# One Trainium2 core, a four-branch mixer and a two-layer block: sums, splits, bias tables and banks moved, and the gated recurrence written in another order

## The chip, the cores and the metric

The kernel runs on one core of one Trainium2 chip. The metric is the device time of one execution in microseconds (us). Within a core five engines run their own instruction queues side by side: PE (matrix multiply), DVE (vector), ACT (scalar, activations), POOL (GpSimd) and SP (here used for weight loads). They meet at semaphores. ACT, POOL and SP can also issue DMA transfers; in the profile such issues stand on ACTq, POOLq and SPq.

## The reference

The input is 256 tokens by 1024 channels, all in float32. Two blocks follow each other.

```python
# first block
h = rmsnorm(x)
z, xbc, dt, b_qkv, c_qkv, c_f, d_q, d_kv, gates = split(h @ w_in)
y_a = mamba2(z, silu(conv4(xbc)), dt)        # decays: exp(cumsum_t - cumsum_s), s <= t
y_b = moba(b_qkv, rel_bias)                  # softmax(q k / 8 + bias[t - s]) v, causal
y_c = forgetting(c_qkv, c_f)                 # softmax(q k / 8 + cum_t - cum_s) v, causal
y_d = sliding_window(d_q, d_kv, sinks, rel_bias)   # window 128, own bias
x = x + (sum_i sigmoid(gates_i) * (y_i @ w_branch_i)) @ w_out
x = x + (silu(h @ w_gate) * (h @ w_up)) @ w_down   # h = rmsnorm(x), width 2816
# second block
x = x + hgrn2(rmsnorm(x));  x = x + swiglu(rmsnorm(x))
y, u = split(rmsnorm(x) @ lru_w_in)          # 1024 and 1024 columns
uc = conv4(u)                                # causal, 4 taps
r, i = sigmoid(uc @ wa + ba), sigmoid(uc @ wx + bx)     # 4 diagonal blocks of 256
a = exp(-8 r softplus(-lam));  b = sqrt(1 - a*a) * (i * uc)
hs = scan(a, b)                              # hs[t] = a[t] hs[t-1] + b[t]
x = x + (hs * gelu(y)) @ lru_w_out
x = x + swiglu(rmsnorm(x));  out = rmsnorm(x)
```

## The kernel before

**Weights and their splitting.** Each float32 product is made of three products in the fast format fp32r: high part by high part, high by low, low by high. All weights come through as 184 units of at most 128 x 2048 numbers, in the order in which PE uses them, over three buffer slots. SP loads a unit in two halves of 512 KB. ACT then rounds each half to `whi` (L947), and the rest `wlo = raw - whi` is made per half by DVE (L1360) or by POOL (L1920); `on_pool` decides which. Before, POOL has the second half of nearly every unit, 161 in all, and DVE the other 207. Every engine's program calls `use(key)` at the place of a unit; there it splits what belongs to it up to two units ahead. A unit of 256 output columns is 48 matmuls of 128x256 on PE (L488, L491, L494); a unit used the other way round has matmuls of 128x512 (L505, L508, L511).

**Order.** Nothing schedules the work at run time: each engine's instruction order is written out by hand. For the three attentions `FOX`, `MOBA` and `SWA` list which weight units ("fills") PE works on between two heads. Head by head PE makes scores (L774, L775, bank 4 or 5 in turn), DVE adds the bias or the mask and takes the maximum (L1637, L1641), ACT takes the exponentials (L1141, L1142), DVE normalises (L1649 to L1652), PE transposes (L782, "turned") and multiplies by the values (L792, L793).

**Sums.** The mamba branch and the forgetting attention need tables of differences of running sums. PE makes 16 rows of sums, ACT copies them to `sums` (L1058), ACT's queue stores them to a DRAM scratch (L1060), waits, and issues eight loads (L1067) that spread each row over 128 partitions (`decs`, `hn`, `wfox`). POOL then masks the tables (L1967). Behind the eight issues in ACT's order stand the copies of the transposed `xst` out of PSUM (L1070), for which PE waits at L692.

**Bias tables.** The bias of the other two attentions depends on t - s. A row of 384 numbers per head is stored to `u_scratch`; two POOL-issued loads of 1 MB (L1989) read it shifted by one per partition, which leaves the key axis mirrored. Eight matmuls with a mirrored identity (`flip`, L761) turn that round, and ACT copies the results back (L1127). These are the fills `win` at the end of the forgetting attention.

**Mamba result.** The normed mamba output is turned (L752, two groups of four transposes) in banks 4 and 5, and ACT and DVE take its high and low part out (L1124, L1619). This is the fill `ym` after the second head of the forgetting attention; scores of the third head use bank 4.

**Recurrence (LRU).** Units `lu0` to `lu3` give u, `ly0` to `ly3` give y, `lg0` and `lg1` hold the gate weights, `lo` is the output product. ACT and DVE make the convolution (L1031, L1490, L1492), its high part (L1289) and low part (L1846); PE multiplies by the gate weights (L915); ACT takes sigmoids (L1302), decays (L1307, L1308) and roots (L1313); DVE scans (L1860); ACT takes gelu (L1318); DVE multiplies (L1867); the product is split again (L1325, L1869) and goes to `lo` (L505).

Of the kernel before, what the change touches and what calls it, by code (L numbers as in the profile page):

```python
# [72 lines left out]
def build(nc, a):  # L73
    V, A, G, T, S = nc.vector, nc.scalar, nc.gpsimd, nc.tensor, nc.sync
    vq, aq, gq, tq, sq = Waits(V), Waits(A), Waits(G), Waits(T), Waits(S)
    with ExitStack() as root:
# [16 lines left out]
        flip = sbuf(root, "flip", [128, 128])  # L93
# [183 lines left out]
        for j in range(4):  # L277
            cols(("lu", j), lw, 1024 + 256 * j, 256)
        cols(("ly", 0), lw, 0, 256)
        lru_gate_unit(0)  # L280
        cols(("ly", 1), lw, 256, 256)
        lru_gate_unit(1)
# [12 lines left out]
        starts = [unit_at[k] for k in (("g", 0, 0), ("hf", 0), ("g", 1, 0), ("lu", 0), ("g", 2, 0))] + [NU]  # L295
# [29 lines left out]
        s_sums, s_masked = sem("sums_stored"), sem("sums_masked")  # L325
# [73 lines left out]
        CONST = {k: i + 1 for i, k in enumerate(["ident", "ones", "flip", "half", "pad", "tri"])}  # L399

        def const(name):
# [3 lines left out]
        FOX = [[("gate", 1, 0)], [("gate", 1, 1), ("ym",)], [("gate", 1, 2)], [("gate", 1, 3)], [("b", 0), ("b", 1)], [("b", 2)],  # L405
               [("b", 3), ("bv",)], [("br", 0, 0)], [("br", 0, 1), ("win", 0)], [("win", 1), ("win", 2)]]
        FOX_REST = [("win", c) for c in range(3, 8)]
# [15 lines left out]

        def windows_of(c):
            return area[:, 3072 + 512 * c:3584 + 512 * c]
# [44 lines left out]
        def tensor_program():  # L470
# [259 lines left out]
            def fill(what):  # L730
# [14 lines left out]
                elif what[0] == "ym":  # L745
                    for c in range(2):
                        b = turn(("ym", c), 4 + c)
# [7 lines left out]
                else:  # L755
                    c = what[1]
                    b = turn(("win", c), next_bank())
                    tq.wait_ge(s_w, 32)
                    tq.wait_ge(*const("flip"))
                    tq.wait_ge(*free(("win", c)))  # L760
                    T.matmul(banks[b][:, :], flip[:, :], windows_of(c), start=True, stop=True).then_inc(s_full[b], 1)  # L761

            def attention(n, fills, rest, inputs):
# [40 lines left out]
                for what in rest:  # L804
                    fill(what)

            windows = [("win", c) for c in range(8)]
            attention(1, FOX, FOX_REST, [("col", "c", j) for j in range(4)] + [("tok", "cv", t) for t in range(2)])
            attention(2, MOBA, [], [("col", "b", j) for j in range(4)] + [("tok", "bv", t) for t in range(2)] + windows)
            attention(3, SWA, [], [("col", "d", 0), ("col", "d", 1), ("col", "dk"), ("dv",)])  # L810
# [125 lines left out]
        def scalar_program():  # L936
# [126 lines left out]
            for rows, h0, parts in ((dec_rows, 0, ((0, 0, 256), (256, 128, 128))), (fox_rows, 8, ((0, 0, 128), (128, 0, 256)))):  # L1063
                for c0, s0, n in parts:
                    for i, heads in enumerate((5, 3)):
                        src = bass.AP(a["sums_scratch"].tensor, (h0 + 5 * i) * 256 + s0, [[0, 128], [256, heads], [1, n]])
                        A.dma_start(rows[i][:, :, c0:c0 + n], src).then_inc(s_spread[h0 // 8], 16)  # L1067
# [30 lines left out]
            def fill(what):  # L1098
# [26 lines left out]
                else:  # L1125
                    aq.wait_ge(*full(*what))
                    A.activation(windows_of(what[1]), bank_of(*what)[:, :], ACT.Copy).then_inc(evacuated(*what), 1)  # L1127

            def attention(n, fills, rest):
# [42 lines left out]
                for what in rest:  # L1172
                    fill(what)

            attention(1, FOX, FOX_REST)
            attention(2, MOBA, [])
            attention(3, SWA, [])
# [113 lines left out]
            def conv_unit(j):  # L1291
                conv_start(j)
                conv_round(j)

            def lru_gates(h):
                use(("lg", h))
                for i, (dst, b0) in enumerate(((ig, 88), (rg, 80))):
                    for n in (2 * h, 2 * h + 1):
# [5 lines left out]
                        t.then_inc(evacuated("lg", i, n), 1)  # L1304
                for c in range(4 * h, 4 * h + 4):
# [14 lines left out]
            def gated(n):  # L1320
                gelu(n)
# [5 lines left out]
            project_pair([("lu", 0), ("lu", 1)], 6, bc_lr, [lambda: None, lambda: None])  # L1327
            use(("lu", 2))
            conv_unit(0)
            use(("lu", 3))  # L1330
            conv_unit(1)
            use(("ly", 0))
            lru_gates(0)
            conv_unit(2)
            conv_unit(3)
            use(("ly", 1))
            lru_gates(1)
            use(("ly", 2))
            for n in range(4):
                root_of(n)  # L1340
            use(("ly", 3))
# [826 lines left out]
```

## Time and profile before

| | |
|---|---|
| median of 3 runs | 1255.49 us (1253.69 to 1258.89) |
| the profiled execution | 1250.67 us |
| its span, first to last instruction | 1249.4 us |
| PE busy | 1194.6 us, 96% |
| DVE, ACT, POOL busy | 682.3, 591.9, 473.1 us |
| TensorE's granted clock, mean | 0.977 |
| moved by DMA | 204.75 MB, mean 164 GB/s |

The profile is of one execution. "Busy" is time in which an engine had an instruction running, so a DVE or POOL that is held up inside an instruction counts as busy. A granted clock of 1.00 is the higher of TensorE's two levels (2.4 GHz), 0.50 the lower (1.2 GHz). A timeline row ends with the engine's idle time before it and the instruction that ended that idle time.

### The profile page before, as it was taken

How to read it: one execution, taken by the hardware profiler on the slowest of the kernel's cores; microseconds unless marked ns; L12 is line 12 of the kernel's file. 1: busy time of each engine (PE TensorE's matmuls, PEld its weight loads, DVE VectorE, ACT ScalarE, POOL GpSimd, SP SyncE). 2: the span in 40 equal slices, each digit the busy share in tenths (PEclk: the TensorE clock that was granted, in tenths of full speed). 3: DMA queues.
4: the chain of work that ended last, by engine and by line, in shares of the span. 5: the costliest groups of instructions: out<-in, count | busy, mean ns of one | idle time of the engine just before them, and what ended most of it. 6: DMA issues, size and time to landing. Idle time of an engine off the chain costs nothing.

```text
span 1249.4 us, 19584 instructions
## 1 busy us (share of the span) xinstructions
PE 1194.6 (96%) x8237; PEld 1096.5 (88%) x8237; DVE 682.3 (55%) x965; ACT 591.9 (47%) x901; POOL 473.1 (38%) x253
## 2 busy tenths in 40 slices
PE   7979999999989999999899999999999769999998
PEld 6979898788878999988898879999889768999986
DVE  5742644366756645334789757433326696633423
ACT  6534544445444554444652345444334674544432
POOL 4345333233231444441654423444423350543440
PEclk9989999999989999999999999999999879999999
DMA  7585465344445666564543435755555333756560
GB/s 240 163 265 154 145 197 144 108 121 125 128 135 152 184 188 187 187 200 143 182 134 135 151 120 171 217 177 185 196 185 173 114 135 118 217 181 187 177 199 34
DMA packets 160833, 204.75 MB, mean 164 GB/s; under 512 B 13535, under 2 KB 135577, under 8 KB 160746
## 3 DMA queue, kind: packets, MB, share of 16 engines
q1 hardware_dynamic: 154650, 193.69, 49.9%
q0 software_dynamic: 1840, 6.64, 1.6%
q10 hardware_dynamic: 4256, 3.16, 0.8%
q8 instruction: 65, 1.06, 0.4%
q14 instruction: 22, 0.18, 0.0%
HBM read 202.38 MB, written 1.09 MB: 163 GB/s over the span
## 4 chain that ended last, share of the span: by engine, by line
PE 78%; DVE 12%; ACT 6%; issue 2%; SPq 1%; ACTq 1%; DMA 0%; POOL 0%; DVEq 0%
PE bank L488 15%; PE bank L491 15%; PE bank L494 15%; PE bank L505 9%; PE bank L511 9%; PE bank L508 9%; ACT whi L947 2%; DVE wlo L1360 2%; DVE sm L1649 1%; PE bank L846 1%; DVE Ss L1780 1%; DVE ring L1651 1%; DVE uc L1490 1%; DVE qT L1774 1%; DVE ring L1637 1%
## 5 line engine op out<-in xcount | busy, mean ns | idle before, releaser
L1920 POOL TENSOR_TENSOR wlo<-raw,whi 128x1024 fp32r<-128x1024 f32 (+1 forms) x161 | 411.6, 2559 | 545.4 <-ACT whi L947 545.4
L947 ACT ACTIVATE whi<-raw 128x1024 fp32r<-128x1024 f32 x368 | 364.9, 1041 | 125.7 <-PE bank L511 117.0
L1360 DVE TENSOR_TENSOR wlo<-raw,whi 128x1024 fp32r<-128x1024 f32 x207 | 277.9, 1352 | 258.9 <-ACT whi L947 257.9
L488 PE MATMUL bank<-hh,whi 128*128 128x256 f32 x1792 | 293.7, 286 | 1.7 <-ACT hh L979 1.7
L491 PE MATMUL bank<-hh,wlo 128*128 128x256 f32 x1792 | 289.4, 284 | 0.9 <-DVE wlo L1360 0.9
L494 PE MATMUL bank<-hl,whi 128*128 128x256 f32 x1792 | 289.0, 284 | 0.0
L488 PEld LDWEIGHTS bank<-hh,whi 128*128 128x128 f32 x1792 | 248.8, 193 | 11.1 <-issue 9.9
L491 PEld LDWEIGHTS bank<-hh,wlo 128*128 128x128 f32 x1792 | 248.3, 193 | 1.4 <-DVE wlo L1360 1.4
L494 PEld LDWEIGHTS bank<-hl,whi 128*128 128x128 f32 x1792 | 248.4, 193 | 0.0
L505 PE MATMUL bank<-whi,gh 128*128 128x512 f32 x264 | 83.4, 397 | 0.0
L511 PE MATMUL bank<-whi,gl 128*128 128x512 f32 x264 | 83.1, 395 | 0.0
L508 PE MATMUL bank<-wlo,gh 128*128 128x512 f32 x264 | 82.5, 393 | 0.0
L1927 POOL TENSOR_TENSOR st<-st,half 128x1 f32<-128x1 f32 x18 | 10.3, 579 | 176.5 <-DVE st L1377 171.2
L1192 ACT ACTIVATE sg<-sg 128x512 f32<-128x512 f32 x33 | 20.8, 632 | 99.5 <-DVE sg L1407 99.5
L1196 ACT ACTIVATE gh<-sg 128x512 fp32r<-128x512 f32 x33 | 20.8, 630 | 88.7 <-DVE sg L1723 88.7
L508 PEld LDWEIGHTS bank<-wlo,gh 128*128 128x128 f32 x264 | 49.6, 188 | 12.3
L511 PEld LDWEIGHTS bank<-whi,gl 128*128 128x128 f32 x264 | 49.5, 188 | 11.6
L505 PEld LDWEIGHTS bank<-whi,gh 128*128 128x128 f32 x264 | 49.2, 188 | 11.7
L505 PE MATMUL bank<-whi,hh 128*128 128x512 f32 (+2 forms) x208 | 56.8, 385 | 0.3 <-ACT hh L1259 0.3
L511 PE MATMUL bank<-whi,hl 128*128 128x512 f32 (+2 forms) x208 | 54.8, 375 | 1.2 <-DVE hl L1680 1.2
L508 PE MATMUL bank<-wlo,hh 128*128 128x512 f32 (+2 forms) x208 | 55.7, 380 | 0.0
L1723 DVE TENSOR_TENSOR sg<-sg,bank 128x512 f32<-128x512 f32 x33 | 22.7, 687 | 60.1 <-PE bank L494 58.0
(296 smaller groups left out, 1319.0 us busy)
## 6 DMA issues: line engine op xcount, KB each, us to landing
raw<-in_ffn_w_in SPq DMA_DIRECT2D x88, 512.0 KB, 3.6
raw<-in_w_in SPq DMA_DIRECT2D x72, 512.0 KB, 3.7
raw<-in_ffn_w_out SPq DMA_DIRECT2D x44, 512.0 KB, 3.2
raw<-in_hgrn_w_in SPq DMA_DIRECT2D x32, 512.0 KB, 4.0
raw<-in_w_ffn_gate SPq DMA_DIRECT2D x22, 512.0 KB, 4.6
raw<-in_w_ffn_up SPq DMA_DIRECT2D x22, 512.0 KB, 4.1
raw<-in_w_ffn_down SPq DMA_DIRECT2D x22, 512.0 KB, 3.3
raw<-in_w_branch SPq DMA_DIRECT2D x16, 512.0 KB, 4.1
```

What stands on the lines that cost most here:

```text
L488: T.matmul(out, wh[:, i, c], xh[:, k, :], start=first and (i, k) == pairs[0], stop=False)
L491: T.matmul(out, wl[:, i, c], xh[:, k, :], start=False, stop=False)
L494: t = T.matmul(out, wh[:, i, c], xl[:, k, :], start=False, stop=last and (i, k) == pairs[-1])
L505: T.matmul(out, xh[:, k, r], wh[:, i, c], start=first and i == 0, stop=False)
L508: T.matmul(out, xh[:, k, r], wl[:, i, c], start=False, stop=False)
L511: tok = T.matmul(out, xl[:, k, r], wh[:, i, c], start=False, stop=last and i == len(ks) - 1)
L947: A.activation(half_of(whi, j, h), half_of(raw, j, h), ACT.Copy).then_inc(s_hi[j % NS][h], 1)
L1192: A.activation(sg[:, j % 2, :], sg[:, j % 2, :], ACT.Silu).then_inc(s_silu, 1)
L1196: A.activation(gh[:, 2 * j:2 * j + 2, :], two(sg[:, j % 2, :]), ACT.Copy).then_inc(s_gh, 1)
L1360: V.tensor_tensor(half_of(wlo, j, h), half_of(raw, j, h), half_of(whi, j, h).bitcast(f32), ALU.subtract).then_inc(s_lo[j % NS][h], 1)
L1723: V.tensor_tensor(s, s, bank_of("col", "u", f, j)[:, :], ALU.mult).then_inc(evacuated("col", "u", f, j), 1)
L1920: G.tensor_tensor(half_of(wlo, j, 1), half_of(raw, j, 1), half_of(whi, j, 1).bitcast(f32), ALU.subtract).then_inc(s_lo[j % NS][1], 1)
```

## The change

1. **Rests.** `on_pool` gives POOL only the second halves of units 2 to 30 behind the start of each of the three feed-forward blocks: 87 instead of 161. The other 74 go to DVE: 48 in the mixer, 16 in HGRN, 10 in the recurrence.
2. **Sums.** The store of the sums and the eight spreading loads are issued from POOL's queue instead of ACT's.
3. **Bias tables.** `flip`, the eight `win` matmuls and their eight ACT copies are gone. POOL issues a DRAM-to-DRAM copy that writes each of the 16 rows 128 times (`u_copies`, 3.1 MB), and the two 1 MB loads read it with a step of 383 numbers per partition, so that the rows come out unmirrored. The fills of the forgetting attention are spread anew; DVE now waits for the loads at the first bias addition of the second attention.
4. **Banks.** The turned mamba output goes to banks 3 and 7 instead of 4 and 5.
5. **Recurrence.** Units and PE's order become lu0 to lu3, lg0, ly0, lg1, ly1, ly2, ly3 (before: lu0 to lu3, ly0, lg0, ly1, lg1, ly2, ly3). On ACT and DVE each convolution is begun one unit sooner, the split of its result is a step of its own (`conv_rest`), the decays are cut off from the sigmoids, gelu follows the roots, and scans stand ahead of the later y units.

```diff
-        def on_pool(j, h):
-            return h == 1 and (j < 2 or j > 2) and all(not u - 2 <= j < u + 2 for u in starts)
+        light = [(unit_at["g", f, 0] + 2, unit_at["g", f, 0] + 31) for f in range(3)]
+        def on_pool(j, h):
+            return h == 1 and any(u0 <= j < u1 for u0, u1 in light)
...
-        FOX = [[("gate", 1, 0)], [("gate", 1, 1), ("ym",)], ..., [("br", 0, 1), ("win", 0)], [("win", 1), ("win", 2)]]
-        FOX_REST = [("win", c) for c in range(3, 8)]
+        FOX = [[("gate", 1, 0)], [("gate", 1, 1), ("ym",)], ..., [("br", 0, 0)], [("br", 0, 1)]]
...
                 elif what[0] == "ym":
-                        b = turn(("ym", c), 4 + c)
+                        b = turn(("ym", c), (3, 7)[c])
...
-                    T.matmul(banks[b][:, :], flip[:, :], windows_of(c), start=True, stop=True).then_inc(s_full[b], 1)
...   (PE, recurrence)
+            lru_gates(0)
             project_columns(("ly", 0), 6)
-            lru_gates(0)
+            lru_gates(1)
             project_columns(("ly", 1), 6)
-            lru_gates(1)
...   (ACT)
-                    aq.wait_ge(*evac("sums"))
-                    A.dma_start(a["sums_scratch"], sums[:, :]).then_inc(s_sums, 16)
-            aq.wait_ge(s_sums, 16)
-            for rows, h0, parts in (...):
-                        A.dma_start(rows[i][:, :, c0:c0 + n], src).then_inc(s_spread[h0 // 8], 16)
...   (DVE, logits)
                     if n == 1:
                         vq.wait_ge(s_masked, 2)
+                    else:
+                        vq.wait_ge(s_w, 32)
...   (POOL)
-            use(("cv", 1), 0)
+            gq.wait_ge(*evac("sums"))
+            G.dma_start(a["sums_scratch"], sums[:, :]).then_inc(s_sums, 16)
+            gq.wait_ge(s_sums, 16)
+            for rows, h0, parts in (...):
+                        G.dma_start(rows[i][:, :, c0:c0 + n], src).then_inc(s_spread[h0 // 8], 16)
...   (POOL, behind the first masks)
-                    use(("gate", 0, 1))
+                    gq.wait_ge(s_u, 16)
+                    G.dma_start(a["u_copies"], a["u_scratch"].rearrange("h (o n) -> h o n", o=1).broadcast_to([16, 128, 384])).then_inc(s_copies, 16)
...
-                        src = bass.AP(a["u_scratch"].tensor, 8 * i * 384, [[1, 128], [384, 8], [1, 256]])
+                        src = bass.AP(a["u_copies"].tensor, 8 * i * 128 * 384 + 127, [[383, 128], [128 * 384, 8], [1, 256]])
```

The first place is ACT's queue at the sums, before; `decs`, `hn` and `wfox` are the tables over 128 partitions, `qkv` holds q and k of the forgetting attention.

```order
L1058 ACTIVATE sums<-bank 16x256 [waits bank_full4]
L1060 DMA sums_scratch<-sums 16x256 [waits bank_evacuated4]
L947 ACTIVATE whi<-raw 128x1024 [waits raw_landed00]
L947 ACTIVATE whi<-raw 128x1024 [waits raw_landed01]
L961 ACTIVATE qkv<-bank 128x512 [waits bank_full1]
L1067 DMA decs<-sums_scratch 128x5x256 [waits sums_stored]
L1067 DMA decs<-sums_scratch 128x3x256
L1067 DMA decs<-sums_scratch 128x5x128
...
L1070 ACTIVATE area<-bank 128x512 [waits bank_full4]
L1070 ACTIVATE area<-bank 128x512 [waits bank_full5]
```

And POOL's queue at the same place, after.

```order
L1946 DMA u_scratch<-ring 16x384 [waits bank_evacuated7]
L1948 DMA sums_scratch<-sums 16x256 [waits bank_evacuated4]
L1955 DMA decs<-sums_scratch 128x5x256 [waits sums_stored]
L1955 DMA decs<-sums_scratch 128x3x256
...
L1955 DMA wfox<-sums_scratch 128x3x256
L1962 AFFINE_SELECT decs<-decs 128x5x128 [waits decay_sums_spread]
...
L1967 DMA u_copies<-u_scratch 2048x1x384 [waits u_stored]
```

On ACT the copies of `xst` into `area` stood behind nine issues and a wait; now they follow the copy of `qkv` directly. The issues stand on POOL ahead of the masks, with no split among them.

The second place is PE's queue at the turned mamba output in the forgetting attention, with bank numbers, before.

```order
L488 MATMUL bank0<-hh,whi 128x256 x4
L491 MATMUL bank0<-hh,wlo 128x256 x4
L494 MATMUL bank0<-hl,whi 128x256 x4
L752 MATMUL bank4<-ident,area 128x128 x4
L752 MATMUL bank5<-ident,area 128x128 x4
L782 MATMUL bank6<-ident,ring 128x128 x3
L774 MATMUL bank4<-qkv0 128x128
L775 MATMUL bank4<-qkv0 128x256
```

And after.

```order
L748 MATMUL bank3<-ident,area 128x128 x4
L748 MATMUL bank7<-ident,area 128x128 x4
L771 MATMUL bank6<-ident,ring 128x128 x3
L763 MATMUL bank4<-qkv0 128x128
L764 MATMUL bank4<-qkv0 128x256
```

The scores of the third head, behind the transposes of the first head's probabilities, no longer go to a bank that the turned mamba output has just filled.

The third place is DVE's queue in the recurrence, from the first convolution to the first gate input factor, before; `up` is u, `uc` the convolution, `cl` its low part.

```order
L1407 TENSOR_TENSOR yg<-bank,bc_lr 128x512
L1360 TENSOR_TENSOR wlo<-raw,whi 128x1024
L1490 SCALAR_TENSOR_TENSOR uc<-up,vec,uc 128x256 x2
L1492 SCALAR_TENSOR_TENSOR uc<-up,vec,uc 128x256
L1490 SCALAR_TENSOR_TENSOR uc<-up,vec,uc 128x256 x2
L1492 SCALAR_TENSOR_TENSOR uc<-up,vec,uc 128x256
L1846 TENSOR_TENSOR cl<-uc,ch 128x512
...
L1851 TENSOR_TENSOR rg<-aT 128x512
```

And after, the last convolution and what follows it.

```order
L1342 TENSOR_TENSOR wlo<-raw,whi 128x1024 x2
L1472 SCALAR_TENSOR_TENSOR uc<-up,vec,uc 128x256 x2
L1474 SCALAR_TENSOR_TENSOR uc<-up,vec,uc 128x256
L1472 SCALAR_TENSOR_TENSOR uc<-up,vec,uc 128x256 x2
L1474 SCALAR_TENSOR_TENSOR uc<-up,vec,uc 128x256
L1830 TENSOR_TENSOR cl<-uc,ch 128x512
L1342 TENSOR_TENSOR wlo<-raw,whi 128x1024 x2
L1835 TENSOR_TENSOR rg<-aT 128x512
L1836 SCALAR_TENSOR_TENSOR rg<-rg,th 128x512
L1835 TENSOR_TENSOR rg<-aT 128x512
L1836 SCALAR_TENSOR_TENSOR rg<-rg,th 128x512
L1389 TENSOR_TENSOR yg<-bank,bc_lr 128x512
```

Before, the first evacuation of y (`yg`) stood ahead of the last two convolutions; now all four are done before it. Where one weight split stood, two stand now.

## Rows read from the trace of the kernel before

**Rows 1.** The page: engines, and the two groups of low-part splits (busy, mean ns).

```profile
PE 1194.6 (96%) x8237; PEld 1096.5 (88%) x8237; DVE 682.3 (55%) x965; ACT 591.9 (47%) x901; POOL 473.1 (38%) x253
...
L1920 POOL TENSOR_TENSOR wlo<-raw,whi 128x1024 fp32r<-128x1024 f32 (+1 forms) x161 | 411.6, 2559 | 545.4 <-ACT whi L947 545.4
...
L1360 DVE TENSOR_TENSOR wlo<-raw,whi 128x1024 fp32r<-128x1024 f32 x207 | 277.9, 1352 | 258.9 <-ACT whi L947 257.9
```

**Rows 2.** Waits of PE: total us, times, longest us.

```profile
PE bank L505 <- DVE cl L1869: 9.6, 1, 9.6
PE bank L915 <- DVE cl L1846: 7.9, 2, 6.8
PE bank L692 <- ACT area L1070: 6.5, 1, 6.5
...
PE bank L782 <- DVE ring L1652: 3.5, 2, 3.0
PE bank L774 <- DVE bl L1619: 3.0, 1, 3.0
```

**Rows 3.** Timeline of ACT at the sums: start, length, instruction, idle before.

```profile
76.45 0.36 ACTq L1060 DMA_DIRECT2D sums_scratch<-sums  x1
...
82.00 2.61 ACTq L1067 DMA_DIRECT2D decs<-sums_scratch  x4
...
89.99 1.09 ACT L1070 ACTIVATE area<-bank 128x512 f32<-128x512 f32 x2 [7.40 <-issue]
```

**Rows 4.** Stretches: length, busy of PE, PEld, DVE, ACT, POOL, granted clock, DMA.

```profile
90.60:97.00 6.40, 6.36 (x19) 5.30 (x20) 3.26 (x4) 3.12 (x5) 6.24 (x5) 0.54 0.90 263
151.30:158.00 6.70, 6.70 (x28) 6.05 (x29) 4.11 (x12) 2.96 (x7) 3.79 (x4) 0.51 0.89 249
361.70:369.70 8.00, 6.98 (x32) 5.88 (x33) 1.90 (x3) 2.76 (x4) 2.46 (x1) 0.57 0.38 131
960.00:1030.00 70.00, 51.58 (x386) 50.26 (x386) 54.32 (x66) 46.33 (x75) 32.95 (x13) 0.84 0.45 146
```

**Rows 5.** Timeline of PE at the full clock.

```profile
158.52 0.64 PE L491 MATMUL bank<-hh,wlo 128*128 128x256 f32 x4
159.00 0.64 PE L494 MATMUL bank<-hl,whi 128*128 128x256 f32 x4
```

**Rows 6.** DMA issues of the page: KB each, us from issue to landing.

```profile
area<-u_scratch POOLq DMA_DIRECT2D x2, 1024.0 KB, 9.5
...
decs<-sums_scratch ACTq DMA_DIRECT2D x1, 640.0 KB, 5.7
...
u_scratch<-ring POOLq DMA_DIRECT2D x1, 24.0 KB, 4.2
```

**Rows 7.** Timeline of POOL, the masks of the decay table.

```profile
90.76 4.24 POOL L1967 TENSOR_SCALAR_AFFINE_SELECT decs<-decs 128x640 f32<-128x640 f32 x4 [9.33 <-DMA decs<-sums_scratch]
```

**Rows 8.** Timelines of ACT and PE, the first use of that table.

```profile
105.73 0.50 ACT L1086 ACTIVATE decs<-decs,am 128x256 f32<-128x256 f32 x1
...
110.79 0.33 PE L707 MATMUL bank<-area,decs 128*128 128x64 f32 x2
```

**Rows 9.** Timeline of PE at the mirrored windows.

```profile
228.63 4.56 PE L761 MATMUL bank<-area,flip 128*128 128x512 f32 x10
234.10 0.46 PE L774 MATMUL bank<-area 64*128 64x128 f32 x2 [0.92 <-ACT area L1127]
```

**Rows 10.** Timelines of POOL and DVE, last heads of the third attention.

```profile
358.39 2.44 POOL L1920 TENSOR_TENSOR wlo<-raw,whi 128x1024 fp32r<-128x1024 f32 x1 [4.86 <-ACT whi L947]
...
358.54 2.30 DVE L1649 TENSOR_TENSOR sm<-sm 128x2 f32<-128x2 f32 x1
360.87 0.17 DVE L1650 RECIPROCAL sm<-sm 128x2 f32<-128x2 f32 x1
```

**Rows 11.** Timeline of DVE, the end of the recurrence.

```profile
1035.58 0.69 DVE L1869 TENSOR_TENSOR cl<-yg,ch 128x512 fp32r<-128x512 f32 x1 [0.70 <-ACT ch L1325]
1036.52 4.63 DVE L1360 TENSOR_TENSOR wlo<-raw,whi 128x1024 fp32r<-128x1024 f32 x4 [0.26 <-ACT whi L947]
```

More of the change, by code:

```diff
@@ L754, in fill, with attention @@
                         tok.then_inc(s_full[b], 1)
[L755 to L760, printed above, removed]
-                    T.matmul(banks[b][:, :], flip[:, :], windows_of(c), start=True, stop=True).then_inc(s_full[b], 1)
-            def attention(n, fills, rest, inputs):
+            def attention(n, fills, inputs):
                 q, k, v, heads_k, window, slot = ATT[n]
@@ L803, in attention @@
                         values(i - 2)
[L804 to L810, printed above, removed]
+            attention(1, FOX, [("col", "c", j) for j in range(4)] + [("tok", "cv", t) for t in range(2)])
+            attention(2, MOBA, [("col", "b", j) for j in range(4)] + [("tok", "bv", t) for t in range(2)])
+            attention(3, SWA, [("col", "d", 0), ("col", "d", 1), ("col", "dk"), ("dv",)])
             branch(3, 0)
@@ L1124, in fill, with attention @@
                         A.activation(bh[:, 0, 2 * c:2 * c + 2, :], two(bank_of("ym", c)[:, :]), ACT.Copy).then_inc(s_bt, 1)
[L1125 to L1129, printed above, removed]
+            def attention(n, fills):
                 slot = ATT[n][5]
@@ L1171, in attention @@
                         values_out(i - 2)
[L1172 to L1177, printed above, removed]
+            attention(1, FOX)
+            attention(2, MOBA)
+            attention(3, SWA)
             branch(3, 0)
@@ L1327, in scalar_program @@
             project_pair([("lu", 0), ("lu", 1)], 6, bc_lr, [lambda: None, lambda: None])
+            conv_start(0)
             use(("lu", 2))
-            conv_unit(0)
+            conv_start(1)
+            conv_round(0)
+            conv_start(2)
+            conv_round(1)
             use(("lu", 3))
-            conv_unit(1)
+            conv_start(3)
+            conv_round(2)
+            use(("lg", 0))
+            conv_round(3)
+            lru_gates(0)
             use(("ly", 0))
-            lru_gates(0)
-            conv_unit(2)
-            conv_unit(3)
+            decays(0)
+            use(("lg", 1))
+            lru_gates(1)
+            decays(1)
             use(("ly", 1))
-            lru_gates(1)
-            use(("ly", 2))
             for n in range(4):
                 root_of(n)
+            use(("ly", 2))
+            gelu(0)
+            gelu(1)
+            gated(0)
+            gelu(2)
+            gated(1)
             use(("ly", 3))
-            for n in range(4):
-                gated(n)
+            gelu(3)
+            gated(2)
+            gated(3)
             add_product(("lo",), 4, 7)
@@ L1668, in attention @@
                         values_rest(i - 2)
-                for what in rest:
-                    fill(what)
-            attention(1, FOX, FOX_REST)
-            attention(2, MOBA, [])
-            attention(3, SWA, [])
+            attention(1, FOX)
+            attention(2, MOBA)
+            attention(3, SWA)
             branch(3, 0)
@@ L1889, in vector_program @@
             input_factor(3)
+            use(("ly", 1))
+            y_of(1)
+            scan(0)
+            scan(1)
             use(("ly", 2))
             y_of(2)
-            scan(0)
-            scan(1)
+            gated(0)
+            scan(2)
+            gated(1)
             use(("ly", 3))
+            scan(3)
             y_of(3)
-            scan(2)
-            gated(0)
-            gated(1)
-            scan(3)
             gated(2)
```

63 lines of the change are left out of this document (29 added, 34 removed).

## The prediction

> **What bounds the kernel now.** I read the page first. PE is busy for 96% of the span, DVE for 55% [rows 1]: only time in which PE stands still, or runs at half speed because of a stop, can be won, unless PE's own work shrinks. Then the waits of PE, longest first [rows 2]. Those that the change touches are L505 on the recurrence's last product (9.6 us), L915 on the convolution (7.9 in two), L692 on the copies of `xst` (6.5), L782 on the normalised probabilities (3.5 in two) and L774 on the turned mamba output (3.0), 30.5 us together. Third, the stretches behind such stops [rows 4]: behind 6.5 us and behind 3.0 us the granted clock is 0.54 and 0.51, near the lower of its two levels, so a stop is paid twice. At full clock four 128x256 matmuls take 0.48 us, the distance of two starts [rows 5], 0.12 each. The trace's own execution took 1250.67 us, 4.8 less than the median of the runs shown, 1255.49; I work the sum against 1250.67 and carry the difference over to the median.
>
> **1. Sums off ACT's queue.** ACT begins to issue at 82.00 and reaches the copies of `xst` at 89.99 [rows 3]; PE waits 6.5 us for them. After the change they follow the copy of `qkv` and the 6.5 us go. In the stretch behind [rows 4] 19 matmuls take 6.36 us; 13 are 128x512, by rows 5 0.24 each, 3.1 together, and the six short ones I put at 0.7, half of the 1.3 they took. So 2.5 more come back if the clock stays up. Gain 9.0.
>
> What is late next is the decay table, since its loads now start from POOL. The sums reach DRAM after 76.45 plus about the 4.2 us of POOL's small store [rows 6], 80.7. Four decay loads are then issued; ACT's took 0.65 each (2.61 for four, rows 3), so the last is out at about 83.3. Landing takes 5.7 us as on ACT's queue, or 9.5 as POOL's 1 MB loads do [rows 6]: 89.0 to 92.8. Masks take 4.24 [rows 7]: 93.2 to 97.0. Before, ACT used the table first at 105.73 and PE at 110.79 [rows 8], when their other work came due; with 9.0 us gone these places come at 96.7 and 101.8. So the table is in time or 0.3 late, and PE has 5 us between. I take 0, and keep 4 for a landing beside full weight traffic (DMA share 0.90 in that stretch).
>
> The Trainium skill bears on this twice. In DMA: Bandwidth & Descriptors, section Anatomy of one DMA — SWDGE (gpsimd) path, it gives such a transfer 2.0 us plus its bytes at 436 GB/s. That would be 2.1 us for the 24 KB store, where the trace has 4.2, so the measurement decides; by the rule the table would be some 6 us earlier still, and the sum the same. The section SWDGE vs HWDGE vs iDMA of that page speaks against the change: GpSimd writes its descriptors into SBUF, and DVE can lock it out of SBUF. No issue in this trace shows it; it stands beside the second rival.
>
> **2. Banks.** The 3.0 us at L774 go, since the third head's scores no longer need a bank that DVE must empty first. Behind it, 28 matmuls take 6.70 us [rows 4]: 24 are 128x256, 2.9 at full clock, the four scores about 0.8. So 3.0 come back with the clock: 6.0. Late next would be banks 3 and 7, which the values of the first heads need; between lie a whole unit of 5.8 us and a transposition, which is the cover. If they bind, the 6.0 are lost again; that is a rival.
>
> **3. Mirrored windows.** Sixteen records of L761 go. Ten take 4.56 us [rows 9], 0.46 each, so 7.3, and the wait of 0.92 behind them, for ACT's last copy: 8.2. They lie on PE with nothing beside them. In their place POOL copies 3.1 MB within DRAM, beside the weight loads. The two 1 MB loads are the same in number and size and are first needed a whole attention later, so the distance hides both, and I cost them at nothing. Without that cover the price is a weight half that stands behind part of the copy: behind a third of it, 1 MB at the mean 164 GB/s of the table, 6.4 us, and a clock that falls by it. I keep 0 to 7.
>
> **4. 74 splits from POOL to DVE.** A POOL split takes 2559 ns on average, a DVE split 1352 [rows 1]. At the end of the third attention DVE's two-column sum takes 2.30 us and ends together with POOL's split at 360.83; the reciprocal of the same shape behind it takes 0.17 [rows 10]. So DVE is held while POOL splits, for about 2.1 us, and a split of its own costs it 1.16 (4.63 for four, rows 11). A moved split then takes 1.0 us less of DVE than it does now. POOL's splits recur every 7.3 us there (4.86 idle and 2.44 busy), that is the pace of a head, set by DVE; a unit of PE's work is 48 x 0.12 = 5.8 and scores, transposes and values some 2.1, 7.9. So in this attention DVE falls back below PE, and the 3.5 us at L782 go. In the stretch behind, 6.98 us of PE's work at 0.57 would be 4.0 at full clock; 3.0 could come back, but part of it waits for ACT and DVE between short matmuls, and I take 1.0. Gain 4.5, bounds 0 and 6.5. In the feed-forward blocks nearly all second halves stay on POOL. HGRN gets 16 splits; where DVE stands in front of its scalings one more split of 1.16 delays PE, and I take 0.7 lost, between 2 lost and 1 won.
>
> **5. Recurrence.** Two waits of 7.9 and 9.6 us [rows 2] lie in one stretch of 70 us in which DVE is busy for 54.3, ACT for 46.3 and PE for 51.6, at a mean clock of 0.84 [rows 4]. The new order ends the first wait early: the convolutions are done before the gates need them, so PE should not stand 6.8 there. If all of that carried through, `lo` would begin 6.8 earlier. But ten more splits, 10 x 1.16, come onto DVE: 65.9 of 70, less the 10 to 20 that POOL no longer holds up (1.0 to 2.1 each). And the tail stays as it is: the last scan and four gated products, each through ACT and back, and behind the last one, at 1035.58, the splits of `lo`'s third and fourth unit, 4.63 us [rows 11]. An earlier start of `lo` then only moves PE's wait to its third unit. I take 0, with bounds -2.5 (two more splits ahead of that unit) and +6.8 (the whole first wait).
>
> **The sum.** 9.0 + 6.0 + 8.2 + 4.5 - 0.7 + 0 = 27.0; I take off 1.5 for new short waits in places that these stops have so far hidden: 25.5. 1250.67 - 25.5 = 1225.2; on the median 1230.0.
>
> **Rivals.**
> *The recurrence gives too* (0.16). For: 17.5 us of waits lie there. Against: DVE's load. 6.8 and the 1.5 more: 1221.7.
> *The sums come late through POOL* (0.13). For: nine issues stand there in a row while DVE splits weights beside them. If each were held for one DVE split, nine times 1.16 us, the table would be masked at 97.0 + 10.4 = 107.4 and ACT and DVE need some of the 5.1 of rows 8 more, say 3.0: PE gets it at 110.4 instead of 101.8, and ACT, standing at its exponential, copies no weights meanwhile. 8.6 and 2.5 for the clock: 1241. Against: the same issues took 0.65 each on ACT. The second rule of the Trainium skill above would work in this way.
> *DVE becomes the bound* (0.07, the slower side). If DVE's long instructions are not POOL's doing, nothing comes back, and each of 24 heads gets 1.16 us on a DVE pace of 7.3: 8.5 against PE's 7.9, 0.6 x 24 = 14 us of waits. Part 4 gives nothing (4.5), the ten splits in the recurrence cost 11.6: 1230 + 30 = 1260, slower than 1255.49. It decides from the point where DVE's work per head is over 7.9 us. Against: 2.30 beside 0.17 [rows 10].
> *The copy takes the weights' time* (0.07): 7 us, 1237. For: it writes as much as six weight halves. Against: half of a busy stretch's DMA time is free (0.45 in the last of rows 4).
> *The clock does not come back, or the banks wait again* (0.07): without 2.5 + 3.0 + 1.0, or without 6.0: 1236. For: both stops have shown it. Against: it needs a stop that the change takes away.
> The forecast itself has 0.50.
>
> **How the numbers follow.** Predicted 1230. The forecast's own range, from the bounds of 1, 4 and 5, is 1221 to 1238. With the rivals, 1215 (all upper bounds, recurrence included) to 1247 (the sums late and a copy in the way). About 0.5%, 6.3 us, is what a measurement can tell here: faster means below 1249.2. All of the cases but DVE's end below that, with some mixtures of two bad ones above: faster 0.86, same 0.08, slower 0.06.
>
> **What would show it.** PE without a wait at the `xst` sums and at the third head's scores, and a granted clock near 1.00 in both stretches; no flip matmuls; DVE's two-column sum at 0.2 us, and no PE wait for the normalised probabilities in the third attention; in the recurrence no long wait at the gates, and a wait at `lo` that has moved behind its second unit. Wrong if PE waits at the mamba products for the decay table, if PE waits for low parts (`wlo`) unit after unit in the attentions, or if weight landings lengthen around the copy.

## The result, and the profile after

| | before | after |
|---|---|---|
| median, first runs | 1254.59 us (4 runs) | 1226.13 us (4 runs, 1224.09 to 1226.61) |
| ratio to before, 95% interval | | 0.9766 [0.9737, 0.9795] |
| run again on another chip | 1251.18 us | 1226.04 us, 0.9801 [0.9777, 0.9825] |
| span of the profiled execution | 1249.4 us | 1225.1 us |

The forecast was 1230 us, with a range of 1215 to 1247; the changed kernel is 2.3% faster, 28.5 us by the medians and 24.3 by the spans. The two differ because the profiled execution before was 3.9 us faster than its median, while the one after stands at its median (1226.38 us). First the page after, against [rows 1].

```profile
span 1225.1 us, 19544 instructions
...
PE 1183.5 (97%) x8221; PEld 1089.2 (89%) x8221; DVE 669.8 (55%) x1039; ACT 587.8 (48%) x893; POOL 298.0 (24%) x187
...
L1342 DVE TENSOR_TENSOR wlo<-raw,whi 128x1024 fp32r<-128x1024 f32 (+1 forms) x281 | 345.5, 1257 | 255.0 <-ACT whi L933 253.9
...
L1908 POOL TENSOR_TENSOR wlo<-raw,whi 128x1024 fp32r<-128x1024 f32 x87 | 223.2, 2565 | 265.8 <-ACT whi L933 265.8
```

DVE has 74 more splits and yet is busy for 12.5 us less: the first sign that POOL's splits had been stretching DVE's other instructions. Next the waits of PE, against [rows 2]; the columns are total us, times, longest.

```profile
PE bank L501 <- DVE cl L1853: 3.6, 1, 3.6
PE bank L501 <- ACT whi L933: 3.3, 1, 3.3
PE bank L649 <- DMA ring<-in_c_onehot: 3.3, 1, 3.3
PE bank L484 <- ACT whi L933: 3.2, 1, 3.2
PE bank L832 <- ACT qT L1196: 3.1, 1, 3.1
PE bank L901 <- DVE cl L1830: 3.1, 2, 2.3
PE bank L487 <- DVE wlo L1342: 2.7, 3, 1.4
```

The waits for the copies of `xst`, for the turned mamba output and for the normalised probabilities are gone. What is left of weight is in the recurrence: L501 is its output product, L901 its gates, and L484 and L487 wait there for the two parts of the last y units' weights.

The stretches behind the three stops of [rows 4] after the change (length, busy of PE, PEld, DVE, ACT, POOL, granted clock, DMA share, GB/s):

```profile
86.90:97.90 11.00, 11.00 (x50) 9.13 (x50) 5.60 (x5) 4.64 (x6) 5.84 (x7) 1.00 1.03 320
141.10:147.80 6.70, 6.70 (x53) 6.35 (x53) 4.67 (x12) 4.30 (x11) 1.81 (x2) 1.00 0.67 185
337.00:345.00 8.00, 6.94 (x54) 6.00 (x53) 4.58 (x6) 3.32 (x6) 0.00 (x0) 1.00 0.46 156
```

The clock stays at 1.00 in all three; where before 28 matmuls ran in 6.70 us, 53 do. The decay table, which now comes through POOL's queue, on the timeline of POOL, ACT and PE:

```profile
79.08 0.50 POOL L1948 DMA_DIRECT2D sums_scratch<-sums  x1 [54.19 <-ACT sums L1044]
81.56 3.36 POOL L1955 DMA_DIRECT2D decs<-sums_scratch  x4 [1.97 <-DMA sums_scratch<-sums]
...
93.42 4.37 POOL L1962 TENSOR_SCALAR_AFFINE_SELECT decs<-decs 128x640 f32<-128x640 f32 x4 [5.16 <-DMA decs<-sums_scratch]
97.73 1.07 POOL L1967 DMA_DIRECT2D u_copies<-u_scratch  x1
...
98.15 0.60 ACT L954 ACTIVATE qkv<-bank 128x512 f32<-128x512 f32 x1 [2.12 <-PE bank L507]
98.64 0.50 ACT L1063 ACTIVATE decs<-decs,am 128x256 f32<-128x256 f32 x1
...
103.70 0.33 PE L703 MATMUL bank<-area,decs 128*128 128x64 f32 x2
```

The masks end at 97.79. ACT takes the table up at 98.64, directly behind its copy of `qkv`, so the table was 0.85 us ahead of ACT and cost nothing; PE's use of it has no idle time in front.

Set against each other, the two traces divide into stretches (from the first instruction of one to that of the next, us):

| stretch | before | after | change |
|---|---|---|---|
| start to the transposes of `xst` | 81.79 | 84.17 | +2.38 |
| to the first product with the decay table | 29.00 | 19.53 | -9.47 (sums) |
| to the turned mamba output | 36.12 | 36.12 | 0 |
| to the fourth head's scores | 15.22 | 9.21 | -6.01 (banks) |
| to the second attention's first scores | 71.97 | 64.14 | -7.83 (windows) |
| to the first feed-forward block | 175.81 | 169.79 | -6.02 (rests) |
| feed-forward block | 191.26 | 191.27 | 0 |
| HGRN | 160.71 | 161.86 | +1.15 |
| feed-forward block | 191.26 | 191.25 | 0 |
| recurrence | 106.87 | 108.38 | +1.51 |
| last feed-forward block to the end | 189.4 | 189.4 | 0 |

The sum is -24.3, the difference of the spans. The mixer won 29.3 us, and the start, HGRN and the recurrence gave 5.0 back. These stretches are what the experiments are read by: a feed-forward block repeats to 0.01 us, while the time of a whole run moves by several us for a reason told under the startup below. A stretch is known for the one profiled execution of a run alone.

### The profile page after: what moved, and what is told of

It is laid out like the page before. It is cut to its first block, busy times and chain, and to the rows that moved or that the text cites. A ratio compares the mean times of both kernels' runs of the same rounds, so it can differ in the third digit from the quotient of the medians.

```text
span 1225.1 us, 19544 instructions
## 1 busy us (share of the span) xinstructions
PE 1183.5 (97%) x8221; PEld 1089.2 (89%) x8221; DVE 669.8 (55%) x1039; ACT 587.8 (48%) x893; POOL 298.0 (24%) x187
## 4 chain that ended last, share of the span: by engine, by line
PE 88%; DVE 5%; ACT 3%; issue 1%; SPq 1%; DMA 1%; POOL 0%; ACTq 0%; DVEq 0%
PE bank L484 18%; PE bank L487 17%; PE bank L490 17%; PE bank L501 9%; PE bank L507 9%; PE bank L504 9%; PE bank L832 2%; DVE wlo L1342 2%; PE bank L781 1%; ACT whi L933 1%; PE bank L764 1%; PE bank L763 1%; PE bank L771 1%; DVE uc L1472 1%; DMA ring<-in_c_onehot 1%
## 5 line engine op out<-in xcount | busy, mean ns | idle before, releaser
L1342 DVE TENSOR_TENSOR wlo<-raw,whi 128x1024 fp32r<-128x1024 f32 (+1 forms) x281 | 345.5, 1257 | 255.0 <-ACT whi L933 253.9
L484 PE MATMUL bank<-hh,whi 128*128 128x256 f32 x1792 | 294.6, 287 | 5.0 <-ACT whi L933 3.2
L487 PE MATMUL bank<-hh,wlo 128*128 128x256 f32 x1792 | 290.1, 285 | 2.7 <-DVE wlo L1342 2.7
L1908 POOL TENSOR_TENSOR wlo<-raw,whi 128x1024 fp32r<-128x1024 f32 x87 | 223.2, 2565 | 265.8 <-ACT whi L933 265.8
L484 PEld LDWEIGHTS bank<-hh,whi 128*128 128x128 f32 x1792 | 249.4, 193 | 14.4 <-issue 13.2
L487 PEld LDWEIGHTS bank<-hh,wlo 128*128 128x128 f32 x1792 | 249.1, 193 | 3.3 <-DVE wlo L1342 3.3
L1915 POOL TENSOR_TENSOR st<-st,half 128x1 f32<-128x1 f32 x18 | 10.3, 579 | 419.0 <-DVE st L1359 393.7
L501 PE MATMUL bank<-whi,gh 128*128 128x512 f32 x264 | 83.4, 397 | 0.0
L501 PEld LDWEIGHTS bank<-whi,gh 128*128 128x128 f32 x264 | 49.2, 188 | 11.7
L501 PE MATMUL bank<-whi,hh 128*128 128x512 f32 (+2 forms) x208 | 56.3, 382 | 0.3 <-ACT hh L1231 0.3
```

Of the source, the lines that this page charges most:

```text
L484: T.matmul(out, wh[:, i, c], xh[:, k, :], start=first and (i, k) == pairs[0], stop=False)
L487: T.matmul(out, wl[:, i, c], xh[:, k, :], start=False, stop=False)
L501: T.matmul(out, xh[:, k, r], wh[:, i, c], start=first and i == 0, stop=False)
L1342: V.tensor_tensor(half_of(wlo, j, h), half_of(raw, j, h), half_of(whi, j, h).bitcast(f32), ALU.subtract).then_inc(s_lo[j % NS][h], 1)
L1908: G.tensor_tensor(half_of(wlo, j, 1), half_of(raw, j, 1), half_of(whi, j, 1).bitcast(f32), ALU.subtract).then_inc(s_lo[j % NS][1], 1)
```

## The experiments

**Sums back on ACT.** In the changed kernel the store and the eight loads go back to ACT's queue.

```diff
-            gq.wait_ge(*evac("sums"))        (POOL: store, wait and eight loads)
+                    aq.wait_ge(*evac("sums"))   (ACT: the same, ahead of the xst copies)
```

> The changed kernel with the store of the sums and the eight spreading loads issued from ACT's queue again. If ACT's issues ahead of the xst copies were what PE waited for, the 6 to 7 us wait at the running sums is back, the granted clock behind it is near 0.55 again, and the time is about 9 us over the changed kernel's 1226: 1235. The rival, that the gain there came from POOL no longer splitting weights in that stretch, expects at most 2 us: 1228.

Measured: 1239.45 us, 0.9909 [0.9893, 0.9926]. ACT and PE on the timeline:

```profile
93.87 1.08 ACT L1056 ACTIVATE area<-bank 128x512 f32<-128x512 f32 x2 [8.88 <-issue]
...
94.52 0.59 PE L688 MATMUL bank<-rates,tri 128*128 128x8 f32 x2 [7.99 <-ACT area L1056]
```

No POOL split stands in that stretch, and the wait is back, even longer, since ACT's issues took 9.3 us here. The stretch grew from 19.53 to 29.86, 10.3 us, and the two profiled executions, 1236.76 and 1226.38, are 10.4 apart. The median lost more than the 9 expected, 13 us; the other three executions were 2.5 to 4.7 us slower than the profiled one, and no profile shows where. The rival falls: with no POOL split beside it, the queue alone brings the stop back.

**Banks 4 and 5 again.**

```diff
-                        b = turn(("ym", c), (3, 7)[c])
+                        b = turn(("ym", c), 4 + c)
```

> The changed kernel with the turned mamba output in banks 4 and 5 again. If the bank alone made the stop, PE waits about 3.0 us at the third head's scores, the clock falls to about half for some 6 us behind it, and the time is 6 us over 1226: 1232. The rival, that the stop was that long only because POOL's splits held DVE and ACT up, expects a wait of 1 to 2 us, no fall of the clock, and 1228.

Measured: 1231.31 us, 0.9834 [0.9819, 0.9849]. PE's wait, and the stretch behind it:

```profile
145.09 0.49 PE L763 MATMUL bank<-qkv 64*128 64x128 f32 x2 [2.57 <-DVE bl L1601]
...
145.10:152.00 6.90, 6.90 (x54) 6.57 (x55) 4.79 (x14) 2.89 (x7) 1.81 (x2) 1.00 0.96 311
```

The stop is there, 2.57 us, and in this execution the clock does not fall: 2.6 us in all where the change had won 6.0. Half of each theory is right here. But the profiled execution was the fastest of four, 1228.50 us at a mean clock of 0.987; the other three took 1231.3 to 1231.8 at 0.984 to 0.985. Whether the clock fell at this place in them, no profile shows.

**Banks 4 and 5 again, with POOL's splits in the attentions again.** To see whether those splits made the stop longer and the clock fall.

```diff
-                        b = turn(("ym", c), (3, 7)[c])
+                        b = turn(("ym", c), 4 + c)
-            return h == 1 and any(u0 <= j < u1 for u0, u1 in light)
+            return h == 1 and (19 <= j < 49 or any(u0 <= j < u1 for u0, u1 in light))
```

> The changed kernel with the turned mamba output in banks 4 and 5 again and, together with it, POOL's 30 splits in the attentions again. Banks alone gave a wait of 2.57 us without a fall of the clock, 2.7 us in all, where the change had won 6.0. If the two parts share the missing 3.4 us (POOL's splits lengthen the stop to 3.0 and the clock falls behind it), the stretch from the turned mamba output to the last transposed probabilities is 197.5 + 3.45 + 6.0 = 207 us. If the missing 3.4 are chance of the clock, it is 197.5 + 3.45 + 2.7 = 203.6, or either value without a longer stop.

Measured in one profile: the stretch from the turned output to the last transposed probabilities is 204.0 us.

```profile
144.47 0.48 PE L763 MATMUL bank<-qkv 64*128 64x128 f32 x2 [3.00 <-DVE bl L1601]
```

```profile
144.50:151.20 6.70, 6.70 (x53) 6.37 (x54) 4.59 (x12) 2.94 (x7) 4.22 (x4) 1.00 0.87 266
```

The stop is 3.00 us, as before [rows 2], but behind it 53 matmuls run in 6.70 us at a granted clock of 1.00, where before it was 28 at 0.51 [rows 4]. So of the 6.0 us, 3.0 are the bank (2.6 without POOL's splits); the other 3.0, the fall of the clock that the kernel before had here, came back in neither profiled execution. That it was owed to this stop is not shown.

**Mirrored windows again.** Loads from the small scratch, eight flip matmuls and eight copies in one row at the end of the forgetting attention, no copy within DRAM.

```diff
+                T.matmul(banks[b][:, :], flip[:, :], windows_of(c), start=True, stop=True).then_inc(s_full[b], 1)
+                A.activation(windows_of(c), bank_of("win", c)[:, :], ACT.Copy).then_inc(evacuated("win", c), 1)
-                    G.dma_start(a["u_copies"], ...)
```

> The changed kernel with the mirrored windows again: both loads read the 16 x 384 scratch, and eight flip matmuls with eight ACT copies stand at the end of the forgetting attention, all in one row; no copy within DRAM. If these lie on PE with nothing beside them, 8 to 9 us are lost: 1234.5. If the DRAM copy costs weight loads something that its absence gives back, 1 to 3 us less: 1232. If the flips were hidden, 1226.

Measured: 1233.78 us, 0.9859 [0.9844, 0.9874]; the stretch grew by 8.00 us.

```profile
214.74 7.13 PE L804 MATMUL bank<-area,flip 128*128 128x512 f32 x16
222.77 0.46 PE L767 MATMUL bank<-area 64*128 64x128 f32 x2 [0.89 <-ACT area L1161]
```

7.13 and 0.89 are all of it. The copy within DRAM gave nothing back by its absence. In the changed kernel it lands 17.1 us after its issue, and the median weight load around it takes 6.4 us (60 to 130 us; KB each, us to landing), from 3.7 before:

```profile
raw<-in_w_in SPq DMA_DIRECT2D x20, 512.0 KB, 6.4
u_copies<-u_scratch POOLq DMA_DIRECT2D x1, 3072.0 KB, 17.1
```

Not all of that is the copy's: without it, in this run, the median is 4.6. The loads issued at 82 to 91 us, beside the eight spreading loads, are slow in both, 11 to 14 us with the copy and 10 to 12.5 without it; the five issued during the copy, at 97 to 110 us, take 10.6 to 14.1 with it and 3.4 to 6.8 without it. PE waited for none of them.

**POOL's splits in the attentions again.** 30 second halves, alone.

```diff
-            return h == 1 and any(u0 <= j < u1 for u0, u1 in light)
+            return h == 1 and (19 <= j < 49 or any(u0 <= j < u1 for u0, u1 in light))
```

> The changed kernel with POOL splitting the second halves of the 30 units of the three attentions (units 19 to 48) again, DVE elsewhere as changed. If POOL's splits hold DVE up, DVE's two-column sums take about 2 us again, PE waits about 3 us for the last normalised probabilities of the third attention and 0.5 at the end of the second, the clock falls behind it, and 4 to 6 us are lost: 1231. The rival, that DVE has long instructions for another reason and the splits cost it their full 1.2 us, expects the same time or up to 2 us less: 1225.

Measured: 1231.73 us, 0.9846 [0.9824, 0.9868]. DVE's groups by shape (busy us, mean ns of one), of the changed kernel and then of this one:

```profile
L1635 DVE TENSOR_SCALAR ring<-ring,sm 128x128 f32<-128x128 f32 x24 | 6.9, 287 | 0.9
...
L1633 DVE TENSOR_TENSOR sm<-sm 128x2 f32<-128x2 f32 x8 | 1.2, 152 | 0.0
```

```profile
L1635 DVE TENSOR_SCALAR ring<-ring,sm 128x128 f32<-128x128 f32 x24 | 30.8, 1285 | 0.8
L1633 DVE TENSOR_TENSOR sm<-sm 128x2 f32<-128x2 f32 x8 | 14.4, 1794 | 0.0
```

The same instructions take 4.5 and 12 times as long when POOL splits beside them. PE waits 2.98 and 0.52 us again, exactly as before, and the stretch to the first feed-forward block grows by 6.1 us. The rival falls.

**The recurrence, order against splits.** Three runs, of one profile each, complete a square: the old order with splits on DVE, the new order with POOL's ten, and both old.

```diff
 (old order)   units, PE, ACT and DVE of the recurrence as in the kernel before
 (POOL's ten)
-            return h == 1 and any(u0 <= j < u1 for u0, u1 in light)
+            return h == 1 and (139 <= j < 149 or any(u0 <= j < u1 for u0, u1 in light))
```

> The changed kernel with the recurrence in the order of before (units, PE, ACT and DVE), all splits in it on DVE. Looked at is the stretch from the second layer norm of the second block's first layer to that of the recurrence's end, 106.87 us before and 108.38 after. If the new order is what costs, the stretch is 105 to 107. If the ten splits on DVE cost and the order gives, it is 110 or more.

> The changed kernel with its new order of the recurrence, but the ten second halves there on POOL as before. If DVE's ten splits cost (10 x 1.16 on the engine that the end waits for), the stretch is 105 to 107 instead of 108.38. If POOL's holding of DVE costs as much as the splits, it stays at 108 to 110.

> The changed kernel with the recurrence both in the old order and with the old ten splits on POOL: the stretch should be that of the kernel before, 106.9, since nothing ahead of it differs in the engines' order. Another length, by more than 0.5 us, would say that what comes before the recurrence changes it.

| recurrence stretch, us | ten splits on POOL | on DVE |
|---|---|---|
| old order | 106.87 (before), 108.01 | 105.34 |
| new order | 114.01 | 108.38, and 107.67 to 108.41 in seven more profiles of this code |
| start of the output product, old order | 75.41, 75.40 | 73.18 |
| start of the output product, new order | 74.80 | 69.72 or 69.73 in all eight |

Both theories fail by half. The order costs: 2.3 to 3.1 us with the splits on DVE, 6 to 7 with POOL's. The splits on DVE do not cost, they give: 1.5 to 2.7 us in the old order, 5.6 to 6.3 in the new. The starts of the output product, counted from the start of the stretch, repeat to 0.01 us and say the same of the splits: on DVE they bring it forward by 2.2 us in the old order and by 5.1 in the new. The new order brings it forward too, by 0.6 and 3.5; what it costs lies behind that start, 37.9 to 39.2 us instead of 31.5 to 32.6. The two old entries differ by 1.1 us, more than expected, and all of it lies behind the product's start, where the granted clock over 8 us is 0.80 before and 0.64 in the run. Waits of PE in the run with the new order and POOL's splits:

```profile
PE bank L501 <- DVE cl L1853: 5.6, 1, 5.6
...
PE bank L501 <- ACT whi L933: 4.3, 1, 4.3
...
PE bank L901 <- POOL wlo L1908: 3.1, 1, 3.1
```

PE waits for a POOL split itself, and 2.0 us longer for the first product than in the changed kernel. DVE is held up: 16 steps of its convolutions (L1472) take 922 ns on average where they take 482 in the changed kernel, four scans (L1844) 1213 where they take 678.

**HGRN's splits back on POOL.**

```diff
-            return h == 1 and any(u0 <= j < u1 for u0, u1 in light)
+            return h == 1 and (86 <= j < 102 or any(u0 <= j < u1 for u0, u1 in light))
```

> The changed kernel with the 16 second halves in HGRN on POOL as before. The HGRN stretch was 160.71 us before and 161.86 after. If DVE's splits stand ahead of ACT's and DVE's scalings there, 160.7; the rival, that the 1.15 us are chance of one execution, expects 161.9 again.

Measured: 160.74. But nine other profiles with the changed kernel's HGRN code have 160.5 to 160.8, and three, the first among them, 161.9 to 162.0. In all twelve PE stops once for 3.08 to 3.10 us, and the clock falls; in those three it stays down for longer. The 16 us around that stop in the changed kernel's first profile and in its second, timed further below:

```profile
594.00:610.00 16.00, 12.92 (x87) 12.76 (x88) 9.35 (x14) 6.53 (x8) 3.94 (x6) 0.79 0.42 134
```

```profile
593.30:609.30 16.00, 12.92 (x98) 12.95 (x98) 10.46 (x19) 7.61 (x10) 4.44 (x7) 0.89 0.39 133
```

The code is the same, so the 1.15 us are chance of an execution, and it is the clock that they are lost by; the 16 splits cost nothing there.

**The recurrence, tightened.** What the changed trace shows there, on PE: the output product starts 69.7 us into the stretch, where it was 75.4 before, works off two units, and then stands.

```profile
997.06 1.19 PE L501 MATMUL bank<-whi,ch 128*128 128x512 f32 x2 [3.60 <-DVE cl L1853]
...
1010.16 1.74 PE L501 MATMUL bank<-whi,ch 128*128 128x512 f32 x2 [3.34 <-ACT whi L933]
...
1013.14 1.06 PE L507 MATMUL bank<-whi,cl 128*128 128x512 f32 x2
1014.00 1.06 PE L501 MATMUL bank<-whi,ch 128*128 128x512 f32 x2
```

5.7 us earlier at its start; from there to the next block 38.7 us instead of 31.5. The third unit waits for its splits, and behind that wait two matmuls take 0.86 us from start to start, twice the 0.45 of full clock. Two moves follow: sigmoids of both halves together with the decays behind them, and the third unit's splits ahead of the last products.

```diff
 (ACT)
-            decays(0)
-            use(("lg", 1))
-            lru_gates(1)
-            decays(1)
-            use(("ly", 1))
+            use(("lg", 1))
+            lru_gates(1)
+            use(("ly", 1))
+            decays(0)
+            decays(1)
...
+            use(("lo", 0))
             gelu(3)
             gated(2)
 (DVE)
+            y_of(0); use(("lg", 1)); use(("ly", 1)); y_of(1)   (ahead of the four input factors)
...
             gated(2)
+            use(("lo", 0))
             gated(3)
```

> The changed kernel with two moves in the recurrence: the sigmoids of both halves follow each other and all decays stand behind them (two ACT table loads of 1.28 us less, and the splits of the last y unit ahead of the decays), and the splits of the third unit of the output product stand ahead of the last gated products on ACT and DVE. If ACT's chain of sigmoids, decays and roots sets the start of the output product, it begins about 67.3 us into the stretch instead of 69.7; if the late splits of its third unit are what gives the early start back, the 3.3 us wait there falls to 2 or less with no fall of the clock, and the stretch is about 103.5 instead of 108.4. The rival, DVE as the bound: the start does not move, and the wait only changes its place; 107.5 to 109.

Measured in one profile: the stretch is 102.67 us, the product starts at 66.5, and the long wait at the third unit is gone; PE's first and longest later stop in that product, and ACT's table loads:

```profile
993.75 1.19 PE L501 MATMUL bank<-whi,ch 128*128 128x512 f32 x2 [7.97 <-DVE cl L1854]
...
1011.52 0.50 PE L504 MATMUL bank<-wlo,ch 128*128 128x512 f32 x1 [0.64 <-DVE wlo L1343]
...
962.15 1.28 ACT L1269 ACT_TABLE_LOAD   x1
975.10 1.28 ACT L1276 ACT_TABLE_LOAD   x1
982.92 1.28 ACT L1282 ACT_TABLE_LOAD   x1
```

The start comes 3.2 us earlier, with two table loads less and the splits moved, so the rival, in which the start does not move, falls. That ACT's chain of sigmoids, decays and roots set the start fits this, but the run also moves DVE's input factors behind the y units, and the two were not separated. The late splits did eat part of the early start: from there to the next block it is 36.1 us instead of 38.7. This version was timed beside the changed kernel.

> The changed kernel as it is, beside the next one on the same chip: ratio to the kernel before 0.977, the recurrence stretch 108.4 us.

> The changed kernel with the sigmoids together, the decays behind them and the splits of the output product's third unit ahead of the last products, timed. One profile had the recurrence stretch at 102.7 us instead of 108.4. If that is the whole difference, the time is 5.7 us under the changed kernel run beside it, a ratio to the kernel before of about 0.972.

Measured: the changed kernel 1226.04 us, 0.9801 [0.9777, 0.9825]; the tightened one 1223.99 us, 0.9773 [0.9750, 0.9796]. In the profiles the stretch is 107.84 and 102.63, 5.2 us apart, but the intervals of the times overlap: by the timed runs the tightened version beats the kernel before and is not shown to be faster than the changed one. The 0.972 expected for it lies outside its interval.

**Why: the startup.** No run was made for it, but the thirteen profiles show it. The transposes of `xst`, ahead of which PE and DVE have the same instructions in all versions of the changed kernel, begin between 82.48 us and 89.65. The stretch from 22 to 30 us in the changed kernel's first profile, in its second, and in the tightened one's second:

```profile
22.00:30.00 8.00, 7.50 (x45) 6.75 (x46) 3.61 (x7) 5.41 (x8) 0.52 (x1) 0.79 0.74 194
```

```profile
22.00:30.00 8.00, 8.00 (x69) 8.00 (x68) 5.45 (x9) 6.61 (x10) 0.52 (x1) 1.00 0.52 150
```

```profile
22.00:30.00 8.00, 6.85 (x27) 5.53 (x28) 2.82 (x6) 4.19 (x7) 0.52 (x1) 0.60 0.72 202
```

PE stops there for a table that comes by DMA, 3.25, 1.66 and 3.87 us, and the clock behind it is 0.79, 1.00 and 0.60. That is not all of it. In all fourteen profiles, the kernel before included, the clock falls a second time, during 48 matmuls of 128x16 or less than 1 us behind them, and PE has no stop there. How long it stays down differs. From 42 to 58 us, the same three profiles:

```profile
42.00:58.00 16.00, 16.00 (x92) 14.12 (x91) 12.07 (x17) 9.91 (x13) 0.00 (x0) 0.89 0.59 182
```

```profile
42.00:58.00 16.00, 16.00 (x68) 13.48 (x69) 9.89 (x15) 7.03 (x8) 0.00 (x0) 0.79 0.69 218
```

```profile
42.00:58.00 16.00, 16.00 (x86) 14.72 (x85) 11.34 (x18) 8.52 (x11) 0.00 (x0) 0.68 0.51 155
```

Between the second and the third of these profiles, the earliest and the latest of the thirteen, the stop ends 2.5 us later, the 50 matmuls behind it take 3.0 longer, and from there to the transposes it is 1.7 more. These 7.2 us are larger than the 5.2 that were to be timed. Whether the changed kernel's startup is slower than that of before stays open: its only profile has 81.79 us, with a stop of 1.79, a clock of 1.00 behind it and of 0.89 from 42 to 58 us.

## Why the prediction was right

1. *Sums*: 9.0 forecast, 9.47 in the traces, 10.3 when undone. The table was forecast in time or 0.3 late and was 0.85 early, on a start 2.4 later. The rival of a DVE that holds up POOL's issues did not come: four issues took 3.36 us, 0.84 each against 0.65 on ACT, and all eight 6.7 us against ACT's 7.9. The rule of the Trainium skill (DMA: Bandwidth & Descriptors, SWDGE vs HWDGE vs iDMA) would bear on it; the trace shows at most this 0.2 us per issue. Issue to landing on POOL's queue:

```profile
decs<-sums_scratch POOLq DMA_DIRECT2D x1, 640.0 KB, 7.2
...
decs<-sums_scratch POOLq DMA_DIRECT2D x1, 192.0 KB, 9.1
...
sums_scratch<-sums POOLq DMA_DIRECT2D x1, 16.0 KB, 2.2
```

   The prediction set 4.2 for the store, from another store in [rows 6]; it took 2.2 (2.7 from ACT's queue before). The loads took 7.2 to 9.1, where 5.7 to 9.5 was set. The figure in the section Anatomy of one DMA — SWDGE (gpsimd) path of that page of the Trainium skill, 2.0 us and the bytes, gives an estimate of 2.0 for the store, which agrees, and of 2.5 to 3.5 for the four table loads, which does not.
2. *Banks*: 6.0 forecast, 6.01 between the traces. The half of it that is the stop is shown by the runs that undo it; the half that is the clock is not, since neither profiled execution lost it. Agreement to 0.01 us is luck, and that a stop "is paid twice" held for this one in the kernel before alone.
3. *Windows*: 8.2 forecast, 7.83, and 8.00 when undone. The cover of the DRAM copy held. A sign that the prediction had named as speaking against it did come, longer weight landings around the copy, but at no price, since PE had its weights in time.
4. *Rests*: 4.5 forecast, 6.02, and 6.1 when undone: the term was undersized. I had taken 1.0 of the 3.0 us of clock behind that stop [rows 4], and 2.5 came back, the 6.02 less the stops of 2.98 and 0.52. HGRN, forecast at -0.7, is 0 but for the chance of the clock.
5. *Recurrence*: 0 forecast, -1.5 between the two traces; against the old code run again behind the changed mixer, 108.01, it is 0.3 to -0.4. Its picture was right: an earlier start of `lo` that then waits at the third unit. The step that failed is "ten more splits, 10 x 1.16, come onto DVE" as the cost that keeps the gain away: that part gave 2 to 6 us, as point 4's own argument would have had it, and the order, splits on DVE, took 2 to 3. That the term came out near 0 is in part luck: the gain of the splits, forecast as a cost, and the cost of the order nearly cancel.
6. The allowance of 1.5 for new waits met a startup that was 2.4 longer, by chance or not; the allowance had not been set for that.
7. The ranges do not follow from the stated bounds: with the lower bound of the recurrence, -2.5, the forecast's own range ends at 1241 and not at 1238, and all upper bounds together give 1218, not 1215.

By its steps the forecast was 25.5 and the traces show 24.3; three terms were right to 0.5 us, and two errors of 1.5 each, rests and recurrence, offset each other. The mechanisms of the sums, the windows and the rests are shown by the runs that undo them, and the agreement of the total is in part luck.

## What to carry to other kernels

An engine that is busy because another holds it up looks like a loaded engine: compare one instruction's duration with and without the other engine working beside it, before counting work that is moved onto it as a cost. A start that an edit moves earlier is worth only as much as what is queued for the second and third unit behind it is ready too. And undo each part by itself before crediting it with a term: a stop that is undone comes back, while the clock behind it may not, so the clock's share of a gain is known only after several profiles.

## What the runs showed of the hardware

A stop of PE does not always bring its clock down. Behind 3.00 us in two kernels the same matmuls ran at 0.51 in one and at 1.00 in the other; behind 2.98 us in the third attention it was 0.57 to 0.58 in all three kernels that had that stop. Behind the same 3.08 us in HGRN it was down for about twice as long in three profiles as in nine others. And it falls without a stop, in all fourteen profiles, during 48 matmuls of 128x16 or right behind them. What tells these apart no run here shows.
